# POOL's half of each weight remainder: eight subtractions of an eighth each in place of one

## The reference

```python
def hybrid_layer(x, ...):
    h = _rms(x) * norm1_g
    proj = h @ w_in                        # 1024 x 7680
    ...                                    # attention, RWKV-7, retention on parts of proj
    mixed = g[:, :, 0] * o_a + g[:, :, 1] * o_b + g[:, :, 2] * o_c
    x = x + mixed @ w_out                  # 1024 x 1024
    h2 = _rms(x) * norm2_g
    x = x + (jax.nn.silu(h2 @ w_ffn_gate) * (h2 @ w_ffn_up)) @ w_ffn_down
    return x                               # run twice
```

## Time and profile before

| what | value |
|---|---|
| median of three executions | 2523.76 us (2520.39 to 2523.99) |
| the profiled execution, its own time | 2515.88 us |
| span of that execution, first to last instruction | 2514.1 us |
| mean granted TensorE clock | 0.895 |
| PE busy | 2000.3 us (80%) |
| DVE busy | 843.5 us (34%) |
| ACT busy | 444.0 us (18%) |
| POOL busy | 346.2 us (14%), of it 317.9 us in L1211 (56 instructions) |

### The profile page before, as it was taken

The page is one execution under the profiler, slowest core; times in us unless marked ns, Lnnn a source line. Parts: engine busy times, 40 slices in busy tenths (PEclk is TensorE's granted clock), DMA queues, the critical chain, the costliest instruction groups (busy, mean ns, idle before and its releaser), DMA issues.

```text
span 2514.1 us, 29575 instructions
## 1 busy us (share of the span) xinstructions
PE 2000.3 (80%) x12744; PEld 1402.5 (56%) x12744; DVE 843.5 (34%) x1186; ACT 444.0 (18%) x429; POOL 346.2 (14%) x75
## 2 busy tenths in 40 slices
PE   6999998999999998999899777656556565556565
PEld 6987778999998777999757564111111111111111
DVE  6854338435756326635336442000000000000001
ACT  3522002334432111332131102000000000000000
POOL 3400013555510002554000000000000000000000
PEclk9999889999999989999999887787787878887877
DMA  6433434656433432566421016999999999999996
GB/s 227 160 134 112 157 126 135 208 161 194 168 134 134 169 146 80 168 191 162 162 101 68 17 69 268 417 417 417 417 418 418 417 418 417 418 417 418 417 417 260
DMA packets 230873, 613.01 MB, mean 244 GB/s; under 512 B 11196, under 2 KB 106684, under 8 KB 197180
## 3 DMA queue, kind: packets, MB, share of 16 engines
q1 hardware_dynamic: 228704, 602.19, 63.0%
q10 hardware_dynamic: 2076, 9.45, 1.0%
HBM read 610.55 MB, written 1.05 MB: 243 GB/s over the span
## 4 chain that ended last, share of the span: by engine, by line
PE 54%; DMA 23%; SPq 11%; DVE 8%; ACT 2%; issue 2%; POOL 0%; ACTq 0%; DVEq 0%; PEldq 0%
SPq L1159 11%; PE PS L1278 10%; DMA work<-in_w_up 8%; DMA work<-in_w_gate 7%; PE PS L1336 7%; PE PS L1330 7%; PE PS L1331 7%; DMA work<-in_w_down 7%; PE PS L559 5%; PE PS L741 2%; PE PS L1260 1%; PE PS L755 1%; DVE hT L2219 1%; DMA ring<-in_w_in 1%; PE PS L1496 1%
## 5 line engine op out<-in xcount | busy, mean ns | idle before, releaser
L741 PE MATMUL PS<-ring,proj 128*32 128x512 f32 x1280 | 194.7, 741 | 125.3 <-DMA ring<-in_w_up 68.5
L1211 POOL TENSOR_TENSOR ring_low<-ring,high_f 128x2048 fp32r<-128x2048 f32 (+1 forms) x42 | 228.5, 5440 | 258.6 <-ACT high_f L1715 258.6
L755 PE MATMUL PS<-work,proj 128*32 128x512 f32 x768 | 132.1, 823 | 105.8 <-DMA work<-in_w_down 105.8
L741 PE MATMUL PS<-work,proj 128*32 128x512 f32 x768 | 130.3, 814 | 101.9 <-DMA work<-in_w_up 65.9
L1278 PE MATMUL PS<-hT,ring 128*128 128x256 f32 x896 | 198.6, 380 | 0.0
L1121 DVE TENSOR_TENSOR proj<-proj,PS 128x512 f32<-128x512 f32 x16 | 11.0, 687 | 545.2 <-PE PS L741 545.2
L1330 PE MATMUL PS<-xh_f,high_f 128*128 128x256 f32 x768 | 184.3, 280 | 5.4 <-DVE hT_low L1910 5.4
L741 PEld LDWEIGHTS PS<-ring,proj 128*32 128x32 f32 x1280 | 38.7, 124 | 267.5 <-DMA ring<-in_w_up 110.4
L1331 PE MATMUL PS<-xh_f,ring_low 128*128 128x256 f32 x768 | 183.8, 278 | 0.0
L1278 PEld LDWEIGHTS PS<-hT,ring 128*128 128x128 f32 x896 | 168.3, 190 | 24.3 <-issue 1.7
L1715 ACT ACTIVATE high_f<-ring 128x4096 fp32r<-128x4096 f32 (+1 forms) x42 | 135.4, 3223 | 262.6 <-PE PS L1336 207.8
(11 more groups left out here) (418 smaller groups left out, 3289.8 us busy)
## 6 DMA issues: line engine op xcount, KB each, us to landing
ring<-in_w_gate SPq DMA_DIRECT2D x96, 1024.0 KB, 19.6
work<-in_w_down SPq DMA_DIRECT2D x96, 1024.0 KB, 19.6
ring<-in_w_in SPq DMA_DIRECT2D x74, 1024.0 KB, 7.3
work<-in_w_up SPq DMA_DIRECT2D x64, 1024.0 KB, 25.2
ring<-in_w_up SPq DMA_DIRECT2D x64, 1024.0 KB, 25.0
work<-in_w_gate SPq DMA_DIRECT2D x32, 1024.0 KB, 23.5
ring<-in_w_down SPq DMA_DIRECT2D x32, 1024.0 KB, 25.3
ring<-in_w_ada SPq DMA_DIRECT2D x24, 1024.0 KB, 6.9
```

What stands on the lines that cost most here:

```text
L741: mm = nt.matmul(PS[32 * j:32 * j + 32, 2 + n // 4, :], XSE[:, k, :], w[:, F_E * kk + 512 * j:F_E * kk + 512 * (j + 1)], start=(k == 0), s ...
L755: mm = nt.matmul(PS[32 * g:32 * g + 32, 5, :], HTE[:, P * c + 32 * d:P * c + 32 * (d + 1)], w[:, D * c + 512 * dh:D * c + 512 * (dh + 1)], ...
L1211: pool.tensor_tensor(ring_low[:, n % RING, c], w, high(n)[:, c].bitcast(F32), ALU.subtract).then_inc(low_pool, 1)
```

## The change

For every slot of `SPLIT` but slot 0, the one subtraction of POOL over half the slot's columns becomes eight over a sixteenth each, one after the other with no wait between them: 256 columns each (176 in the down slots). The last of the eight raises `low_pool`, so what PE waits for counts as before. 56 instructions become 448. Nothing changes on any other engine.

```diff
                 for j in range(lo, hi):
                     n = SPLIT[j]
-                    c = slice(width(n) // 2, width(n))
-                    w = ring[:, n % RING, c]
                     pool.wait_ge(high_ready, len(SPLIT) * l + j + 1)
-                    pool.tensor_tensor(ring_low[:, n % RING, c], w, high(n)[:, c].bitcast(F32), ALU.subtract).then_inc(low_pool, 1)
+                    half, piece = width(n) // 2, width(n) // 16
+                    for at in range(half, width(n), piece):
+                        c = slice(at, at + piece)
+                        ins = pool.tensor_tensor(ring_low[:, n % RING, c], ring[:, n % RING, c], high(n)[:, c].bitcast(F32), ALU.subtract)
+                    ins.then_inc(low_pool, 1)
```

## The result

The changed kernel takes 2542.12 us in the median, against 2522.13 of the kernel before on the same chip: 1.0084 times as long, 95% interval 1.0071 to 1.0097. The medians differ by 20 us; the ratio, an estimate from all executions and not the quotient of the medians, comes to 21. The forecast was 24 us more.

The account below looks back on a forecast made before the run. The prediction took POOL, 14% busy, to be on the edge of PE's path at nearly every slot. Its terms summed to 12.0 us per layer, 24 us for two layers, so 2523.8 + 24 = 2548 us; range 2530 to 2566.

Parts of the forecast that it names:

- What bounds: At nearly every slot POOL's end comes last before PE's product; distance above 0.16 us is slack.
- Alternation: Between pieces DVE gets the port, so DVE waits at most 0.65 us and POOL waits for each DVE instruction.
- rival A: POOL doesn't let go between pieces, DVE is held as long as now: 9 us slower, 2533; chance 0.16.
- The walk through the queue ahead of `w_out`: Before `w_out`, where DVE is last, PE starts 1.7 us earlier per layer; bounds 0 and 7.
- The fixed cost: Each added POOL instruction costs 0.08 us, so eight instead of one add 0.57 us per slot.
- C, dear pieces: Alternation with pieces costing 0.2 us each: 2562; sign: pieces over 0.65 us apart; chance 0.10.
- gate-and-up slots 13 to 20: No DVE work beside the pieces: 0.2 us lost every other slot, four times, 0.8 us per layer.
- The down slots: Seven slots without slack, 0.57 us each, paid once in three slots: 1.3 us per layer.
- The early slots: DVE instructions get between POOL's pieces and delay PE: 3.3 us at slot 3, 2.9 at slot 5, 2.8 at slot 7.
- The start of layer 1: At a layer's start DVE waits less in slot 1, then alternates with pieces: taken as 0, bounds +1 and -2.
- The clock: New PE gaps of 3 us may lower the clock: one loss of 1.7 us per layer, bounds 0 and 5.

Follow-up runs that it names:

- e6: Kernel before with DVE taking 15 of 16 parts of each slot's low part, POOL one of 16 in one instruction: 2499.45 us, ratio 0.9904.
- e8: Kernel before with POOL's share cut to a quarter of each slot, in eight pieces, DVE taking three quarters: 2505.12 us, ratio 0.9934.
- e4: Changed kernel with four pieces per slot in place of eight: 2521.84 us, 1.0006 of the kernel before.
- e5: Changed kernel, eight pieces, with DVE's token shift cut from 256 tokens to 8: 2531.8 us, 1.0033 of the kernel before.
- e9: Kernel before, one POOL instruction, with DVE's token shift cut from 256 tokens to 8: 2513.22 us, ratio 0.9964.
- e1: Kernel before with eight pieces in slots 1 to 7 alone: 2535.3 us, ratio 1.0075.
- e3: Kernel before with eight pieces in the two slots of `w_out` alone: 2513.67 us, ratio 0.9975.

## Why the prediction was right, and where it was not

**What bounds.** Right: the waits view named nobody, and the distance from POOL's end to PE's start told where POOL was last. In the changed kernel that distance is at its minimum at nearly every slot that was named, with one more, slot 12, and at slot 1. Two readings were wrong. The smallest distance is 0.10 us, not 0.16: it stands twice in the trace of the kernel before (down slots 25 and 27 of the split list, layer 1), so every slack was 0.06 larger, 0.46 for the steady gate-and-up slots. And 0.06 was the slack of one down slot, not of seven. In layer 1 the distances of the seven go from 0.10 to 0.56, and in six of layer 2's POOL isn't last at all: it got the port first and took 3.21 us, and DVE waited and ended 1.5 us after it, at 1161.66 against 1160.17 (timeline of DVE, kernel before):

```profile
1156.99 4.67 DVE L1898 TENSOR_TENSOR ring_low<-ring,high_f 128x1408 fp32r<-128x1408 f32 x1 [2.30 <-ACT high_f L1715]
```

**Alternation.** Right, and it was the step with the least behind it. L1958 with 1.8 us, L2219 with 1.2, POOL's 9.4 us: rival A, held as long as now, needed 5 us and more at L1958. The walk through the queue ahead of `w_out` gave a gain of 1.7 us; on the way from ACT's rounding to the product the traces show 2.2 in layer 1 and 2.9 in layer 2.

**The fixed cost was mis-sized.** 0.08 us per piece was taken from the intercept of a line; it is 0.14, 1.00 us per slot in place of 0.57. The line went through two long instructions, of 2048 and 1408 columns, and was used far from them. At 256 columns it gives 0.65 us; a POOL instruction of that width with nothing beside it takes 0.74 (timeline of e6):

```profile
25.67 0.74 POOL L1211 TENSOR_TENSOR ring_low<-ring,high_a 128x256 fp32r<-128x256 f32 x1 [24.76 <-ACT high_a L1715]
```

In a series, pieces of 88, 128, 176, 256, 352 and 512 columns (e8, the changed kernel, e4) start 0.33, 0.42, 0.52, 0.70, 0.90 and 1.25 us apart: 2.15 ns per column and 0.15 us. By the prediction's own sign, over 0.65 us from one piece to the next, this is "C, dear pieces", with a price between the forecast's 0.08 and C's 0.2. Where nothing falls beside the pieces this is all there is: gate-and-up slots 13 to 20 lost 2.4 us in both layers (forecast 0.8; (1.00 - 0.46) x 4 = 2.2, and under 0.1 at each slot between). The down slots lost 3.2 us in layer 1 (forecast 1.3) and 1.8 in layer 2, where DVE was last before. The forecast had them pay once in three slots; in layer 1 it was nearer to every other. The estimate from the Trainium skill ("GPSIMD Engine Reference", section "Performance pitfalls for Q7 kernels"), two read commands per piece at 0.085 us, comes to 1.2 us per slot; that is nearer than mine, and still above the 1.00 that was measured. That a loss is paid every other gate-and-up slot is right: in the changed kernel PE falls back by 0.5 us at every second gate-and-up slot and by less than 0.1 between.

**The early slots.** Slot 3 cost 2.7 us (forecast 3.3), slot 5 2.7 (2.9), slot 7 2.9 (2.8), the clock 1.1 in slot 6 (1.7). The walk added DVE's work and part of the fixed cost; e5 and slot 3 speak for the fixed cost hiding under DVE's work altogether. The start of layer 1, taken as 0, gained 1.55. In layer 2 the way to slot 7 lost only 4.6 us: before, PE waited there for ACT and ran 6.8 us at 1.2 GHz, afterwards 3.4 and without the wait, so 3.6 us came back at slot 6. The wait (waits view, 674:711) and a windows row behind it, kernel before:

```profile
PE PS L1395 <- ACT proj L1724: 1.7, 1, 1.7
...
682.00:690.00 8.00, 7.92 (x25) 6.09 (x26) 2.92 (x2) 7.34 (x11) 3.99 (x1) 0.59 0.01 4
```

This step missed that a delay of PE can cover a wait that stood behind it, and that the two layers, though of the same code, have different waits.

**The clock.** Its place was not where I put it alone: behind the 5.9 us gap ahead of `w_out` the stage of `w_out` and feed-forward lost another 1.9 us (layer 1) and 1.4 (layer 2). Nothing in the sum stood for it.

So 24 was near 20 by errors that cancel: the trace has 9 us less than forecast in the early slots of both layers, and 8 us more in the feed-forward stages. The profiled execution became 28 us longer, not 24, of which 5.7 fall into the stage after the layers, which the change doesn't touch and whose length differs from trace to trace by that much (1311.4 to 1317.5 in these runs).

## What to carry to other kernels

Two engines that lock each other out are one engine: what counts is the sum of their times, so give the work to the one that is quicker per column (here DVE, up to 15 of 16 parts) and leave the other only what it doesn't hold up. To cut a long instruction into pieces doesn't shorten that sum, it lengthens it by a fixed cost per piece and hands the waiting to the other side; do it only in the stage where the held engine is last (here `w_out`, -6.6 us), and ask in every other stage how much slack the cut one has. An engine that is 14% busy can be last at almost every step; compare its ends with the starts of those it serves, slot by slot, since a wait that fits in the gap is named nowhere.

## What the runs showed of the hardware

**Hand-over.** A POOL and a DVE instruction that exclude each other take turns at instruction boundaries in both directions: DVE's nearly empty instructions between eight pieces leave POOL at 7.71 us, the same as with no neighbours.

**Middle-sized pieces can be the worst.** At the start of layer 1, eight short DVE instructions take 8.45 us against pieces of 512 columns, 6.84 against 256, and 5.2 with one POOL instruction of 2048 (L1938 in the timeline of before; 3.7 in layer 2). With one long instruction only the first of the eight waits, with pieces most of them do. This is one place in one trace of each kernel.

**The cost of one more POOL instruction.** Some 0.15 us from start to start beside 2.15 ns per column, for pieces of 88 to 512 columns with two SBUF inputs.

**The clock hides more than the change.** The stage from slot 7 to `w_out` has PE work that no run but for its last microseconds changes, and its length goes with the granted clock. Windows rows of three kernels (before, e4, e9):

```profile
113.50:401.10 287.60, 266.97 (x1591) 219.81 (x1590) 138.43 (x228) 54.73 (x69) 19.87 (x6) 0.95 0.37 132
```

```profile
118.50:400.00 281.50, 260.28 (x1590) 216.62 (x1590) 136.88 (x228) 54.68 (x69) 22.82 (x12) 0.97 0.38 137
```

```profile
113.00:403.50 290.50, 268.07 (x1590) 221.21 (x1589) 138.38 (x228) 54.74 (x69) 19.98 (x6) 0.94 0.36 130
```

281.5 us at 0.97, 287.6 at 0.95, 290.5 at 0.94. e9 is the kernel before in this stage and 2.9 us longer. One trace against another is thus good to some microseconds in such a stage. At full clock it is good to a tenth in the gate-and-up slots (slot 12 to slot 20 takes 90.0 us in before, e1, e3 and e9) and to about a microsecond in the down slots; the medians of several executions are needed for the whole, the slot-by-slot starts for the parts. Why the clock falls more often in one execution than in another is left open.
